# Recurrence units: score products in turn over four corners, level sums on TensorE, backward log decays on GpSimd

## The reference, cut to what matters

```python
def step(state, inp):                  # once per chunk, for each direction
    qc, kc, vc, lf = inp
    b = jnp.cumsum(lf, axis=2)
    o_inter = jnp.einsum('bhtk,bhkv->bhtv', qc * jnp.exp(b), state)
    diff = jnp.where(incl[:, :, None], b[:, :, :, None, :] - b[:, :, None, :, :], -jnp.inf)
    att = jnp.einsum('bhtk,bhsk,bhtsk->bhts', qc, kc, jnp.exp(diff))
    o = o_inter + jnp.einsum('bhts,bhsv->bhtv', att, vc)
...
```

## Time and profile before

| | us |
|---|---|
| median of 3 runs | 4500.78 |
| lowest, highest run | 4494.38, 4502.87 |
| span of the profiled execution | 4493.7 |
| own time of the profiled execution | not listed apart; the lowest run stands 0.7 above the span |
| units of layer 0 (12) in the profile | 264.37 to 374.35 |
| units of layer 1 (8) in the profile | 2800.54 to 2874.44 |

### The profile page before, as it was taken

One profiled execution on the slowest core, in us unless ns is written; L12 is line 12 of the kernel. 1 busy time (PEld: TensorE's weight loads), 2 busy tenths in 40 slices (PEclk: granted clock), 3 DMA queues, 4 the chain that ended last, 5 costly groups with the idle time before them and its releaser, 6 DMA issues. The chain is left out here.

```text
span 4493.7 us, 66652 instructions
## 1 busy us (share of the span) xinstructions
PE 3975.2 (88%) x22101; PEld 3427.2 (76%) x22101; DVE 3658.5 (81%) x7139; ACT 1844.1 (41%) x3320; POOL 1121.6 (25%) x1095
## 2 busy tenths in 40 slices
PE   7978978957899999999999878898947899999998
PEld 6965447856788888888888757644746899999998
DVE  4386783899979999999999954766799799999998
ACT  3324632103734444444444343353306544444443
POOL 0000000004933443443444300000008433333332
PEclk9958998966999999999999988699968999999999
DMA  4100221114699999999999911012115899999997
GB/s 177 52 15 23 73 91 38 57 52 131 189 355 370 376 383 372 377 379 376 375 375 375 340 47 57 14 43 80 63 50 147 332 371 370 371 375 372 373 370 282
DMA packets 246472, 1019.00 MB, mean 227 GB/s; under 512 B 16992, under 2 KB 115392, under 8 KB 146000
## 3 DMA queue, kind: packets, MB, share of 16 engines
q0 software_dynamic: 85968, 603.75, 34.7%
q1 hardware_dynamic: 160320, 413.17, 25.5%
HBM read 964.36 MB, written 52.43 MB: 226 GB/s over the span
## 5 line engine op out<-in xcount | busy, mean ns | idle before, releaser
L1206 POOL DMA_INDIRECT rows<-rows,pick_i x512 | 797.5, 1558 | 1156.8 <-DVE y_tok L2359 644.8
L487 PE MATMUL psA<-h_hi,split_hi 128*128 128x448 f32 (+3 forms) x2768 | 977.0, 353 | 120.6 <-DVE xT L2338 47.4
L1762 DVE TENSOR_TENSOR split_lo<-raw,split_hi 128x1024 fp32r<-128x1024 f32 x596 | 727.8, 1221 | 353.2 <-ACT split_hi L1247 342.8
L487 PE MATMUL psA<-h_lo,split_hi 128*128 128x448 f32 (+3 forms) x2768 | 953.9, 345 | 0.0
L487 PE MATMUL psA<-h_hi,split_lo 128*128 128x448 f32 (+3 forms) x2768 | 953.9, 345 | 0.0
L1247 ACT ACTIVATE split_hi<-raw 128x1024 fp32r<-128x1024 f32 x596 | 628.4, 1054 | 329.3 <-DMA raw<-expert_pairs 150.6
L487 PEld LDWEIGHTS psA<-h_hi,split_hi 128*128 128x128 f32 x2768 | 527.8, 191 | 208.0 <-issue 133.2
L2347 DVE CUSTOM_DVE_ANT_1 rows<-rows,h_wide 128x1024 f32<-128x1024 f32 x512 | 624.4, 1220 | 12.4 <-DMA rows<-rows,pick_i 10.1
L2359 DVE SCALAR_TENSOR_TENSOR y_tok<-rows,pick_w,y_tok 128x1024 f32<-128x1024 f32 x444 | 568.9, 1281 | 5.9
L487 PEld LDWEIGHTS psA<-h_hi,split_lo 128*128 128x128 f32 x2768 | 528.0, 191 | 37.0
L487 PEld LDWEIGHTS psA<-h_lo,split_hi 128*128 128x128 f32 x2768 | 529.2, 191 | 33.7 <-issue 0.2
(11 more groups left out here) (303 smaller groups left out, 6538.4 us busy)
## 6 DMA issues: line engine op xcount, KB each, us to landing
raw<-expert_pairs SPq DMA_DIRECT2D x256, 1024.0 KB
gates<-g_buf SPq DMA_DIRECT2D x24, 2048.0 KB, 8.7
raw<-tiles SPq DMA_DIRECT2D x84, 512.0 KB, 3.4
raw<-mod_tiles SPq DMA_DIRECT2D x80, 512.0 KB, 3.4
g_in<-gates POOLq DMA_DIRECT2D x32, 896.0 KB
g_in<-gates POOLq DMA_DIRECT2D x32, 640.0 KB
mod_w<-mod_pairs SPq DMA_DIRECT2D x8, 1024.0 KB, 17.4
rows<-rows,pick_i POOLq DMA_INDIRECT x512, 8.5
```

What stands on the lines that cost most here:

```text
L487: ins = nc.tensor.matmul(out_, lhsT, rhs, start=start, stop=stop)
L1206: nc.gpsimd.indirect_dma_start(rows[l][:, b, :], None, (rows0, rows1)[l], bass.IndirectOffsetOnAxis(pick_i[:, u:u + 1], 0))\
L1762: V.tensor_tensor(split_lo[:, n % SPLIT].rearrange("p k n -> p (k n)"), raw[:, n % RAW, :], split_hi[:, n % SPLIT].rearrange("p k n -> p ( ...
```

## The change

PE's `scores` goes through the corners in turn for each level, and the products are the same 32. `scores` on DVE becomes one product with the masks out of psV, over all eight slots (the far one's mask is all ones), and the sum over levels moves to PE: `output` now makes 28 + 4 products of 64x64 in place of 8, accumulating in psA. It waits for `psum_V_free` in place of `att_ready`. The backward half of `log_decays` moves to POOL, and ACT waits for both halves. `masks` grows by one slot of 64 columns; `attm` takes 8192 bytes of a partition in place of 3584.

```diff
 PE, scores(u):
-                for hd in range(2):
-                    r = slice(64 * hd, 64 * hd + 64)
-                    for half in range(2):
...
-                        for li in range(1, NLB):
-                            mm(psV[hs, f + hd, (li - 1) * 64:li * 64], lvl[r, 0, li, hs], lvl[r, 1, li, hs], True, True)
-                        mm(psV[hs, f + hd, 384:448], kk_sum[r, hp, cs], cq[r, hp, cs], True, True)
-                        ins = mm(psV[hs, f + hd, 448:512], lvl[r, 0, 0, hs], lvl[r, 1, 0, other], True, True,
-                                 last=hd == 1 and half == 1)
+                score_full[l].append(seen.n[psum_V_free])
+                corners = [(hd, half) for half in range(2) for hd in range(2)]
+                rows = [slice(64 * hd, 64 * hd + 64) for hd in range(2)]
+                for li in range(1, NLB):
+                    for hd, half in corners:
+                        mm(psV[rows[half], f + hd, (li - 1) * 64:li * 64], lvl[rows[hd], 0, li, rows[half]],
+                           lvl[rows[hd], 1, li, rows[half]], True, True)
+                for hd, half in corners:
+                    cs = slice(tt * P + 64 * half, tt * P + 64 * half + 64)
+                    mm(psV[rows[half], f + hd, 384:448], kk_sum[rows[hd], hp, cs], cq[rows[hd], hp, cs], True, True)
+                for hd, half in corners:
+                    ins = mm(psV[rows[half], f + hd, 448:512], lvl[rows[hd], 0, 0, rows[half]],
+                             lvl[rows[hd], 1, 0, rows[1 - half]], True, True, last=hd == 1 and half == 1)
 PE, output(u, fo):
-                pe.wait_ge(att_ready, seen.upto(att_ready))
-                for hd in range(2):
-                    h = 2 * hp + hd
-                    for half in range(2):
-                        hs = slice(64 * half, 64 * half + 64)
-                        for far in range(2):
-                            c0 = t * P + 64 * (half ^ far)
-                            ins = mm(psA[64 * hd:64 * hd + 64, fo + half, c0:c0 + 64], ci[hs, tt, h * 64:(h + 1) * 64],
-                                     att[hs, u % 2, far, hd], half == 1, half == 1 or far == 1, last=True)
+                pe.wait_ge(psum_V_free, score_full[l][u] + 4)
+                corners = [(hd, half) for half in range(2) for hd in range(2)]
+                for li in range(NLB):
+                    for hd, half in corners:
...
+                        mm(psA[64 * hd:64 * hd + 64, fo + half, c0:c0 + 64], ci[hs, tt, h * 64:(h + 1) * 64],
+                           attm[hs, u % 2, hd, li], half == 1 and li == 0, half == 1 and li == NLB - 1, last=True)
+                for hd, half in corners:
...
+                    ins = mm(psA[64 * hd:64 * hd + 64, fo + half, c0:c0 + 64], ci[hs, tt, h * 64:(h + 1) * 64],
+                             attm[hs, u % 2, hd, NLB], half == 1, True, last=True)
 POOL, after the DMA of w_uq:
+            units_before = sum(len(recurrence_units(j)) for j in range(l))
+            for u, (hp, _, tt, _) in enumerate(recurrence_units(l)):
+                lvl = lvls[u % 3]
+                if u == 2:
+                    pool.wait_ge(state_ready, l + 1)
+                if u >= 3:
+                    pool.wait_ge(unit_passed, units_before + u - 2)
+                b = cb[2 + hp][:, tt * P:(tt + 1) * P]
+                for li, m in enumerate(LEVELS):
+                    ref = b.rearrange("p (b t) -> p b t", t=2 * m)[:, :, m:m + 1]
+                    ins = nc.gpsimd.tensor_tensor(halves(lvl[:, 1, li], 0, m, m - NLB * P), halves(b, 0, m, m),
+                                                  ref.unsqueeze(2).broadcast_to([P, P // (2 * m), 2, m]), ALU.subtract)
+                ins.then_inc(lvl_raw_b, 1)
 ACT, decays(u):
                 act.wait_ge(lvl_raw, seen.upto(lvl_raw))
+                act.wait_ge(lvl_raw_b, seen.upto(lvl_raw_b))
 DVE, log_decays(u):
+                b = cb[hp][:, tt * P:(tt + 1) * P]
                 for li, m in enumerate(LEVELS):
-                    for d in range(2):
...
-                        ins = V.tensor_tensor(to_k_then_q if d == 0 else to_q_then_k, halves(b, 0, m, m),
-                                              ref.unsqueeze(2).broadcast_to([P, P // (2 * m), 2, m]), ALU.subtract)
+                    ref = b.rearrange("p (b t) -> p b t", t=2 * m)[:, :, m - 1:m]
+                    ins = V.tensor_tensor(halves(lvl[:, 0, li], 0, m, NLB * P + m), halves(b, 0, m, m),
+                                          ref.unsqueeze(2).broadcast_to([P, P // (2 * m), 2, m]), ALU.subtract)
 DVE, scores(u):
-                V.tensor_tensor(attm[:], psV[:, f:f + 2, 0:448].rearrange("p h (l t) -> p h l t", l=NLB),
-                                masks.unsqueeze(1).broadcast_to([P, 2, NLB, 64]), ALU.mult).then_inc(dve_chain, 1)
-                dve.wait_ge(dve_chain, seen.upto(dve_chain))
                 if u >= 2:
                     dve.wait_ge(att_used, seen.upto(att_used))
-                V.tensor_copy(att[:, u % 2, 1], psV[:, f:f + 2, 448:512]).then_inc(psum_V_free, 2)
-                V.tensor_reduce(att[:, u % 2, 0], attm[:].rearrange("p h l t -> p h t l"), AX.X, ALU.add).then_inc(att_ready, 1)
+                V.tensor_tensor(attm[:, u % 2], psV[:, f:f + 2].rearrange("p h (l t) -> p h l t", l=SLOTS),
+                                masks.unsqueeze(1).broadcast_to([P, 2, SLOTS, 64]), ALU.mult).then_inc(psum_V_free, 2)
                 dve.wait_ge(psum_V_free, seen.upto(psum_V_free, 2))
-                dve.wait_ge(att_ready, seen.upto(att_ready))
```

More of the change, by code:

```diff
@@ L44 @@
 NLB = 7
+SLOTS = NLB + 1
 TB = 32
@@ L215, in build_program @@
     lvl_raw = semaphore("lvl_raw")
+    lvl_raw_b = semaphore("lvl_raw_b")
     lvl_exp = semaphore("lvl_exp")
     qk_ready = semaphore("qk_ready")
-    att_ready = semaphore("att_ready")
     att_used = semaphore("att_used")
@@ L307, in build_program @@
     iota16 = const(TOPK)
-    masks = const(NLB * 64).rearrange("p (l t) -> p l t", l=NLB)
+    masks = const(SLOTS * 64).rearrange("p (l t) -> p l t", l=SLOTS)
     resets = const(T + 1)
@@ L335, in build_program @@
     av_sq = in_r("av_sq", 12288, [P, NTT, 256])
-    attm = in_r("attm", 70656, [P, 2, NLB, 64])
+    attm = in_r("attm", 70656, [P, 2, 2, SLOTS, 64])
     kk_sum = in_r("kk_sum", 6144, [P, 2, T])
@@ L341, in build_program @@
     au = place("au", [P, 2, T], F32, HB + 6144)
-    att = place("att", [P, 2, 2, 2, 64], F32, HB + 6144)
     cg = place("cg", [P, 2, T], F32, HB + 12288)
@@ L475, in build_program @@
     out_bank = [[] for _ in range(DEPTH)]
+    score_full = [[] for _ in range(DEPTH)]
     @block.tensor
@@ L653, in scores @@
                 pe.wait_ge(psum_V_free, seen.upto(psum_V_free, 2))
-                for hd in range(2):
-                    r = slice(64 * hd, 64 * hd + 64)
-                    for half in range(2):
-                        hs = slice(64 * half, 64 * half + 64)
-                        other = slice(64 - 64 * half, 128 - 64 * half)
-                        cs = slice(tt * P + 64 * half, tt * P + 64 * half + 64)
-                        for li in range(1, NLB):
-                            mm(psV[hs, f + hd, (li - 1) * 64:li * 64], lvl[r, 0, li, hs], lvl[r, 1, li, hs], True, True)
-                        mm(psV[hs, f + hd, 384:448], kk_sum[r, hp, cs], cq[r, hp, cs], True, True)
-                        ins = mm(psV[hs, f + hd, 448:512], lvl[r, 0, 0, hs], lvl[r, 1, 0, other], True, True,
-                                 last=hd == 1 and half == 1)
+                score_full[l].append(seen.n[psum_V_free])
[11 more added lines that the diff above has]
+                             lvl[rows[hd], 1, 0, rows[1 - half]], True, True, last=hd == 1 and half == 1)
                 ins.then_inc(psum_V_full, 2)
@@ L677, in output @@
                 mm(o_, states[:, 2 + hp, tt], lf[:, 2 + hp, own_tokens], False, False)
-                pe.wait_ge(att_ready, seen.upto(att_ready))
-                for hd in range(2):
-                    h = 2 * hp + hd
-                    for half in range(2):
-                        hs = slice(64 * half, 64 * half + 64)
-                        for far in range(2):
-                            c0 = t * P + 64 * (half ^ far)
-                            ins = mm(psA[64 * hd:64 * hd + 64, fo + half, c0:c0 + 64], ci[hs, tt, h * 64:(h + 1) * 64],
-                                     att[hs, u % 2, far, hd], half == 1, half == 1 or far == 1, last=True)
+                pe.wait_ge(psum_V_free, score_full[l][u] + 4)
+                corners = [(hd, half) for half in range(2) for hd in range(2)]
+                for li in range(NLB):
+                    for hd, half in corners:
+                        h = 2 * hp + hd
+                        hs = slice(64 * half, 64 * half + 64)
+                        c0 = t * P + 64 * half
+                        mm(psA[64 * hd:64 * hd + 64, fo + half, c0:c0 + 64], ci[hs, tt, h * 64:(h + 1) * 64],
```

(9 more changed lines are left out.)

## The result

| us | before | changed |
|---|---|---|
| median of the runs taken together | 4497.58 (4 runs) | 4439.77 (3 runs) |
| ratio, 95% interval | | 0.9867 (0.9851 to 0.9882) |
| time and span of the profiled execution | not listed apart, 4493.7 | 4436.05, 4434.2 |
| units of layer 0, of layer 1 | 109.98, 73.90 | 83.88, 54.20 |
| attention of layer 0, of layer 1 | 247.71, 205.21 | 246.65, 200.86 |

A fourth run of the changed kernel took 9637 us, a disturbance seen in no other run, and is left out. The kernel is 57.8 us faster; 47 were forecast. "Units" is from the first product with `kk` to the end of the last `collect`, "attention" from there to the end of DVE's last TENSOR_REDUCE out of `psV`. The units give 45.8 us of it and attention 5.4. The rest of the span's 59.5, some 8 us, lies between layers and behind, where nothing was changed.

A forecast was written before the change was run, and what follows sets the result against it. DVE was taken to set the pace in the units, PE close behind. Turns 52.8, first masks 1.3 and tails 8.0 gave 62 us, less 15 for POOL as the pace: 47 us, 4500.8 to 4454 us, range 4435 to 4481.

The forecast's parts named there:

- rival 1: POOL keeps up with DVE in the units: turn 5.53 us, saving 62 us, 4438.7 us; chance 0.33.
- 62 us: Saving with DVE as the pace: 52.8 from full turns, 1.3 from first masks' waits, 8.0 from tails.
- DVE's turn: DVE's work per unit: log decays 1.65, decayed products 2.58, scores 1.30, so 5.53 us, 3.30 less than before.
- PE's turn: PE's work per unit: score products 2.0, state products 1.15, products out of `attm` 1.7, so 4.9 us, under DVE's 5.53.
- rival 3: TensorE becomes the pace in the units: 0.053 us a record, turn 8.3 us, saving about 10 us; chance 0.06.
- Tails: From the last decayed product of each layer: 16.2 to 12.0 us and 16.35 to 12.5, together 8.0 us less.
- Nothing gained elsewhere: Outside the units' turns and tails: earlier log decays, larger `masks` load, ACT and POOL's DMAs change the time by 0.
- POOL stands still for DVE, and DVE does not wait: In the units POOL waits through DVE's 4.2 us a turn with both inputs in SBUF; DVE loses nothing.
- POOL's turn: POOL's work per unit: 4.2 us blocked plus 2.6 for seven subtractions, 6.8 us; beyond 5.85 it costs 15 us.
- rival 2: In the units DVE waits for POOL's 0.37 us seven times a turn: turn 8.1 us, saving 21 us, 4480; chance 0.09.
- The figure of 0.60 for a TENSOR_SCALAR: Nearest profile row for POOL's subtraction, a 128x128 instruction taking 0.60 us, used in pricing one POOL instruction.
- my 0.50: Price taken for one POOL subtraction in the backward log decays: 0.50 us alone, 0.37 of it needing DVE quiet.

The follow-up runs named there:

- POOL only writes: Changed kernel with POOL's seven subtractions a unit replaced by memsets of the same outputs, backward log decays left out: 4425.14 us, ratio 0.9827.

## Why the prediction was right or wrong

The time, 4440 for 4454, lies in the range, on the side of the saving of rival 1, and the sign is right. The mechanism given for the distance from 62 us is not.

**DVE's turn: right.** Where POOL does not read, it is 5.53 us to the hundredth. That exactness is in part luck: its three parts are 1.64, 2.63 and 1.26 us for 1.65, 2.58 and 1.30, and the 0.08 us behind the mask product are 0.11 in the earlier trace rows (283.25 - 283.14). Right too is that PE stays behind DVE in the changed kernel's turns.

**PE's turn: right at the lower clock**, 1.92 us of score products for 2.0 and 1.99 for `attm`'s. The clock was not foreseen: I took the earlier trace rows's 0.50 as given, and PE's own new work raised it to 0.71. On the pace this changed nothing. PE's turn is 5.06 us at the lower level (287.10 to 292.16) for 4.9, so 0.47 under DVE's 5.53 where I had 0.6, and 2.9 at the upper (280.32 to 283.21). The rate that rival 3 doubted holds: (1.99 - 0.31) / 63 = 0.027 us a record over 64 records, for 0.028.

**Tails: under-sized.** From the last group of products layer 0 takes 10.65 us (337.52 to 348.17) for 12.0, layer 1 9.39 (2811.43 to 2820.82) for 12.5, 4.5 us in all, as the products of the last units run at the upper level (1.16 us for 64 in place of 1.99). In the kernel where POOL only writes the tails are 10.0 and 10.3 us. That is the distance from the 62 us to the 66.0 that the units gave where POOL only writes (183.88 - 117.89).

**Nothing gained elsewhere: wrong by 5.4 us.** Attention got shorter by 1.06 and 4.35, in layer 1 with the clock at its start at 1.00 where it was 0.63 before (the window 2874.44 to 2882 of before). The 4.35 stand in all three profiles of the changed kernel; the 1.06 of layer 0 do not (246.65, 246.70 and 248.36 for 247.71).

**POOL: the step that failed** is "POOL stands still for DVE, and DVE does not wait". I forecast POOL's turn at 6.8, as the pace, for 15 us. Measured: POOL's instruction is 0.39 us alone and 0.45 beside DVE's, its seven take 2.9, and DVE waits, 0.19 us per pair. The prediction's own sign of rival 2 is there, DVE's short subtractions longer than 0.29 us: 0.48 to 0.51 where they meet POOL's. The direction is rival 2's, the size half its 0.37, and it hits nearly all of the 16 x 7 pairs: 20 us in place of 41. So the 6.8 us that I forecast for a turn and the 6.78 measured from mask to mask agree by chance: the first is POOL held up by DVE, the second DVE held up by POOL.

The reading that misled is that of the earlier trace rows, where DVE's instruction met POOL's and kept its 0.41 us. It was no accident of one pair. In the kernel before, 187 of the 192 instructions of L2309 overlap one of POOL's, and all of them last 0.41 to 0.43 us (256 columns) or 0.54 to 0.55 (384), as the five do that meet none, whether DVE's began 0.2 us before POOL's or up to 0.5 behind. The mistake was to let POOL's TENSOR_SCALAR there stand for a TENSOR_TENSOR beside short instructions of DVE. Why DVE loses nothing in the one case and 0.19 us in the other, no run tells: no TENSOR_SCALAR of POOL's was tried in the units. What holds in both is that a long DVE instruction holds POOL up (one of POOL's subtractions lasts 1.24 us, from 272.39, beside the product with `cq`, which itself goes from 1.08 to 1.30). The figure of 0.60 for a TENSOR_SCALAR was no bound for a TENSOR_TENSOR either: it is 0.39.

The Trainium skill (SBUF — State Buffer, Who interferes with whom) says that whichever of the pair issued first holds the shared port for its whole instruction and the other fully blocks. The alternation agrees with holding by the instruction. The Trainium skill (GPSIMD Engine Reference, Performance versus the Vector engine) gave an estimate of 0.28 us for POOL's 128 columns before the start-up; measured is 0.39 with it, and it was the better guide than my 0.50.

Whether the block is full the traces leave open. POOL's subtractions alone start 0.36 us apart and DVE's 0.203, so a pair of full instructions would need 0.56 us, and takes 0.41. But the start-up of one may lie beside the other's work. Without start-ups DVE's columns need 0.133 us, as the prediction worked out, which leaves 0.28 of the 0.41 for POOL's.

So the sum was 62 - 15 = 47, and the measured terms are 66 - 20 + 5.4 = 51 in the stages that I can name, with the rest of the 58 to 59 us in the difference between runs. That the time lies in the range is thus in part luck: the 20 us that DVE loses were not in the sum, the 15 us for POOL as the pace did not come, and tails and attention gave some 9 us more than forecast.

**Part by part** (units, us under the 183.9 of before): order of the scores 9.7, sum on TensorE 25.3, log decays on POOL 16.7 (each alone); the first two together 43.1, all three 46.3. The third part, worth 16.7 alone, is worth 3.2 behind the other two.

## What to carry to other kernels

Before work is moved from VectorE to GpSimd, list what VectorE does in the time that it will run: beside instructions with one input in PSUM or with one input only it was nearly free here, beside short ones with two SBUF inputs each pair can give back as much as the move saved (0.19 us of 0.203 here). One added wait that shifts GpSimd's work to the harmless stretch took 8 of 20 us back in the units. A price read from another kind of GpSimd instruction (TENSOR_SCALAR for TENSOR_TENSOR) was wrong in size and in who waits. And a stretch's TensorE clock is no constant of the stage: products added to TensorE raised it for themselves (0.50 to 0.69), so PE's turn is worth pricing at both levels. What it does for the stage behind has to be measured: with 0.71 in the units attention of layer 1 was 4.35 us shorter than before, with 0.93 (four products in line) 4.4 us longer.

## What the runs showed of the hardware that I had not expected

- VectorE and GpSimd alternate, instruction by instruction. The loss to VectorE's instruction with two SBUF inputs (128 columns) is 0.19 us beside a GpSimd TENSOR_TENSOR, 0.09 beside a COPY with one input, and about none beside a MEMSET. Beside a GpSimd TENSOR_SCALAR 187 instructions of VectorE with two SBUF inputs (256 and 384 columns) lost nothing. With one input in PSUM, or one input, VectorE loses nothing.
- GpSimd's TENSOR_TENSOR of 128 columns, in strided halves down to single columns, is 0.39 us alone and 0.36 from start to start, its MEMSET 0.20.
- Products of 64x64 in the four corners of the array run side by side as long as few of one corner stand in line: at the upper clock 1.09 us for 32 with one in line, 1.23 with two, 2.62 with four, 3.29 with eight; at the lower 1.92, 2.08 and, with eight, 5.92.
- The mean granted clock of the units went from 0.50 to 0.71 with all three parts, 0.55 and 0.57 with the new order alone, 0.69 and 0.67 with the sums alone; it stayed at 0.50 with the log decays alone on GpSimd, and was 0.89 and 0.93 with four products in line.
